# Stick-breaking attention: three score buffers, scores three heads ahead, taken between the exponents

## The reference, cut to what matters

```python
z = einsum('bhqd,bhkd->bhqk', qi, k) * scale
strict = kpos[None, :] < qpos[:, None]
u = where(strict, log_sigmoid(-z), 0.0)
tail = cumsum(u, axis=3, reverse=True) - u
w = where(strict, exp(log_sigmoid(z) + tail), 0.0)
out = einsum('bhqk,bhkd->bhqd', w, v)
```

## Time and profile before

| | us |
|---|---|
| median of 3 runs (lowest, highest) | 1932.29 (1927.04, 1932.38) |
| profiled execution: time, span | 1924.79, 1923.0 |
| busy PE / DVE / ACT, share of the span | 92% / 42% / 31% |
| first scores start, value rows start (in the span) | 929.08, 941.39 |
| loop over heads: first `rest`, last `values` matmul | 971.35, 1083.26 |

### The profile page before, as it was taken

The page is one execution under the profiler, slowest core; times in us unless marked ns, Lnnn a source line. Parts: engine busy times, 40 slices in busy tenths (PEclk is TensorE's granted clock), DMA queues, the critical chain, the costliest instruction groups (busy, mean ns, idle before and its releaser), DMA issues. The chain is left out here.

```text
span 1923.0 us, 27361 instructions
## 1 busy us (share of the span) xinstructions
PE 1759.9 (92%) x11698; PEld 1353.9 (70%) x11698; DVE 803.9 (42%) x1351; ACT 590.3 (31%) x988; POOL 61.5 (3%) x86
## 2 busy tenths in 40 slices
PE   6999989999989988738999899989999989999997
PEld 3883445666655655427765699889998889999886
DVE  3865566111110110144357467343236545444333
ACT  4323422100000000045557533443323333232222
POOL 1001000000000000020000000000000000000000
PEclk9999989999999999978899899899999999999999
DMA  9856525899999999951110111122233032322321
GB/s 371 273 170 192 228 102 197 336 427 425 427 428 427 426 427 427 416 191 41 38 45 23 45 45 35 54 67 88 88 97 123 1 99 89 109 89 88 110 88 44
DMA packets 111217, 355.38 MB, mean 185 GB/s; under 512 B 8663, under 2 KB 71405, under 8 KB 97399
## 3 DMA queue, kind: packets, MB, share of 16 engines
q1 hardware_dynamic: 106342, 343.89, 46.8%
q0 software_dynamic: 4224, 9.33, 1.4%
q10 hardware_dynamic: 530, 0.40, 0.1%
HBM read 330.21 MB, written 23.33 MB: 184 GB/s over the span
## 5 line engine op out<-in xcount | busy, mean ns | idle before, releaser
L1663 PE MATMUL psum<-parts_memory 128*128 128x256 f32 (+3 forms) x1136 | 346.8, 305 | 10.6 <-PEq L1882 3.3
L1665 PE MATMUL psum<-parts_memory 128*128 128x256 f32 (+3 forms) x1136 | 342.8, 302 | 0.0
L1664 PE MATMUL psum<-parts_memory 128*128 128x256 f32 (+3 forms) x1136 | 342.7, 302 | 0.0
L1562 DVE TENSOR_TENSOR parts_memory<-fixed,parts_memory 128x1024 fp32r<-128x1024 f32 x139 | 166.9, 1222 | 212.1 <-ACT parts_memory L1554 212.1
L1663 PEld LDWEIGHTS psum<-parts_memory 128*128 128x128 f32 x1136 | 218.0, 192 | 20.5 <-DVE parts_memory L1562 4.6
L1664 PEld LDWEIGHTS psum<-parts_memory 128*128 128x128 f32 x1136 | 217.9, 192 | 7.0
L1665 PEld LDWEIGHTS psum<-parts_memory 128*128 128x128 f32 x1136 | 217.5, 191 | 6.8
L1663 PE MATMUL psum<-mix_parts,parts_memory 128*128 128x256 f32 (+2 forms) x664 | 206.4, 311 | 4.7 <-PEq L2613 4.0
L1664 PE MATMUL psum<-mix_parts,parts_memory 128*128 128x256 f32 (+2 forms) x664 | 207.1, 312 | 0.0
L1665 PE MATMUL psum<-mix_parts,parts_memory 128*128 128x256 f32 (+2 forms) x664 | 206.4, 311 | 0.0
L1554 ACT ACTIVATE parts_memory<-fixed 128x1024 fp32r<-128x1024 f32 x139 | 143.2, 1055 | 120.7 <-PE psum L1665 109.6
(11 more groups left out here) (414 smaller groups left out, 2387.3 us busy)
## 6 DMA issues: line engine op xcount, KB each, us to landing
fixed<-in_w_exp_gate_dram SPq DMA_DIRECT2D x19, 2048.0 KB, 29.8
fixed<-in_w_exp_up_dram SPq DMA_DIRECT2D x19, 2048.0 KB, 31.1
fixed<-in_w_exp_down_dram SPq DMA_DIRECT2D x19, 2048.0 KB, 31.4
fixed<-in_w_in_dram SPq DMA_DIRECT2D x36, 1024.0 KB, 5.4
attention_memory<-in_w_exp_up_dram SPq DMA_DIRECT2D x14, 2048.0 KB, 31.1
attention_memory<-in_w_exp_down_dram SPq DMA_DIRECT2D x14, 2048.0 KB, 31.4
attention_memory<-in_w_exp_gate_dram SPq DMA_DIRECT2D x14, 2048.0 KB, 29.8
fixed<-in_w_mod_dram SPq DMA_DIRECT2D x8, 2048.0 KB, 9.0
```

What stands on the lines that cost most here:

```text
L1562: dve.tensor_tensor(out, raw, high.bitcast(F32), ALU.subtract).then_inc(self.low_ok, 1)
L1663: pe.matmul(out, x(0), w(0), start=start, stop=False)
L1664: pe.matmul(out, x(0), w(1), start=False, stop=False)
L1665: return pe.matmul(out, x(1), w(0), start=False, stop=stop)
```

## The change

There are now three buffers `zbuf` and none for `wbuf`, whose place they take together with one shared `tail`. The log term is written to `sbuf`, the softplus over it, and the exponents over the softplus, so that z stays whole until the weights are written over z. The pieces have their own banks (0, 1, 2, and 7 for "2", "3" and "m" together), `linear_query` moves from bank 7 to bank 6. `scores` run three heads ahead, all six pieces together, and DVE takes the scores of head h+2 between the exponents of head h. `linear_query` comes after `values`. The weights are made by two exps, and on ACT the log term of head h+2 comes before the outputs of head h are collected. POOL's memset covers three buffers. The core of the diff:

```diff
-    PIECES = (("0", 0, 0), ("x", 1, 1), ("1", 0, 0), ("2", 1, 1), ("3", 1, 7), ("m", 1, 2))
+    PIECES = (("0", 0, 0, 0), ("x", 1, 1, 0), ("1", 0, 2, 0), ("2", 1, 7, 0), ("3", 1, 7, 2 * P), ("m", 1, 7, 3 * P))
+    RESTS = (2, 3, 1, 0, "x", "m")
...
                 if r == 3:
-                    pe.wait_ge(z_sb, 11)
+                    pe.wait_ge(z_sb, 12)
...
             def linear_query(h):
                 w = parts.use(pe, GQ_AT + h // 2)
-                if h:
-                    pe.wait_ge(q_sb, h)
-                pe.wait_ge(z_sb, 6 * min(h + 1, HEADS - 1) + 5)
-                turned(pe, psum[:, 7, 0:HALF], w, x, (h % 2) * HALF, HALF).then_inc(q_ps, 1)
+                turned(pe, psum[:, 6, META:META + HALF], w, x, (h % 2) * HALF, HALF).then_inc(q_ps, 1)
...
-                    before = {0: 6 * h - 2, 2: 6 * h + 2, 4: 6 * h - 1, 5: 6 * h}.get(n, 0)
-                    if before > 0:
-                        pe.wait_ge(z_sb, before)
-                    if i == "3" and h >= 2:
-                        pe.wait_ge(q_sb, h - 1)
+                    if h and n < 4:
+                        pe.wait_ge(z_sb, 6 * (h - 1) + n + 1 if n < 3 else 6 * h)
...
                 pe.wait_ge(sp_ok, h + 1)
-                for n, i in enumerate((3, 2, 1, 0, "x", "m")):
-                    before = {0: 6 * h - 1, 1: 6 * h - 2, 2: 6 * h + 1, 3: 6 * h + 2, 4: 6 * h + 3, 5: 6 * h}[n]
-                    if before > 0:
-                        pe.wait_ge(arg_ok, before)
+                for n, i in enumerate(RESTS):
+                    bank = 3 + n % 2
+                    if h or n > 1:
+                        pe.wait_ge(arg_ok, 6 * h + n - 1)
...
             def values(h):
-                pe.wait_ge(w_ok, h + 1)
+                pe.wait_ge(w_ok, 2 * h + 1)
                 if h:
                     pe.wait_ge(pv_sb, 3 * h)
...
+                pe.wait_ge(w_ok, 2 * h + 2)
...
+                if h:
+                    pe.wait_ge(q_sb, h)
...
+            scores(2)
             for h in range(HEADS):
                 rest(h)
+                if h + 3 < HEADS:
+                    scores(h + 3)
+                values(h)
                 linear_query(h)
-                if h + 2 < HEADS:
-                    scores(h + 2, (0, 1))
-                values(h)
-                if h + 2 < HEADS:
-                    scores(h + 2, (2, 3, 4, 5))
...
+            def weights(h):
+                z, t = zbuf[:, h % 3, :], sbuf[:, h % 2, :]
+                act.wait_ge(arg_ok, 6 * h + 4)
+                act.activation(z[:, 0:Z_META], t[:, 0:Z_META], ACT.Exp).then_inc(w_ok, 1)
+                act.wait_ge(arg_ok, 6 * h + 6)
+                act.activation(z[0:META, Z_META:], t[0:META, Z_META:], ACT.Exp).then_inc(w_ok, 1)
...
             for h in range(HEADS):
-                act.wait_ge(arg_ok, 6 * h + 6)
-                act.activation(wbuf[:, h % 2, :], zbuf[:, h % 2, :], ACT.Exp).then_inc(w_ok, 1)
-                act.wait_ge(q_ps, h + 1)
-                act.activation(gq[:, h // 2, (h % 2) * HALF:(h % 2 + 1) * HALF], psum[:, 7, 0:HALF], ACT.Copy,
-                               scale=DK ** -0.5).then_inc(q_sb, 1)
+                weights(h)
+                if h + 2 < HEADS:
+                    log_term(h + 2)
                 take(h)
                 if h % 2:
                     parts.high(act, GQ_AT + h // 2 + W_SLOTS)
-                if h + 2 < HEADS:
-                    log_term(h + 2)
...
-                if h >= 2:
-                    dve.wait_ge(w_ok, h - 1)
+                if h >= 3 and n == 0:
+                    dve.wait_ge(pv_ps, 3 * (h - 2))
+                dve.wait_ge(z_ps, 6 * h + (n + 1 if n < 3 else 6))
...
             for h in range(HEADS):
-                exponents(h)
+                for n, pieces in enumerate(((), (0,), (1, 2), (3, 4, 5), (), ())):
+                    exponent(h, n)
+                    if h + 2 < HEADS:
+                        for piece in pieces:
+                            take_scores(h + 2, piece)
+                if h:
+                    add_later_keys(h - 1)
                 if h < 2:
                     parts.low(dve, GQ_AT + 2 + h)
                 elif h % 2 == 0:
                     parts.low(dve, GQ_AT + h // 2 - 1 + W_SLOTS)
                 if h + 1 < HEADS:
                     softplus(h + 1)
-                if h + 2 < HEADS:
-                    take_scores(h + 2, (0, 1))
-                add_later_keys(h)
-                if h + 2 < HEADS:
-                    take_scores(h + 2, (2, 3, 4, 5))
+            add_later_keys(HEADS - 1)
```

More of the change, by code:

```diff
@@ L1867, in stick_breaking @@
     o += 2560
[L1868 to L1871, removed]
+    tail = arena[:, o:o + Z_ALL]
+    o += Z_ALL
+    zbuf = arena[:, o:o + 3 * Z_ALL].rearrange("p (i n) -> p i n", i=3)
+    o += 3 * Z_ALL
     k2 = [src[:, at:at + K_ROWS] for src, at in [(big, 6336 + K_ROWS * n) for n in range(4)] +
@@ L1983, in values @@
             def values(h):
-                w = wbuf[:, h % 2, :]
-                pe.wait_ge(w_ok, h + 1)
+                w = zbuf[:, h % 3, :]
+                hc = slice(h * HD, (h + 1) * HD)
+                first, second = psum[0:HD, 5, :], psum[HD:2 * HD, 5, :]
+                pe.wait_ge(w_ok, 2 * h + 1)
                 if h:
                     pe.wait_ge(pv_sb, 3 * h)
[L1988 to L1995, removed]
+                for out, i in ((first, 0), (second, 1), (second, 2)):
+                    pe.matmul(out[:, i * P:], v[:, i, hc], w[:, Z_AT[i]:Z_AT[i] + (TT - i) * P], start=(i < 2), stop=False)
+                pe.wait_ge(w_ok, 2 * h + 2)
+                pe.matmul(first, v[:, TT, hc], w[:, Z_META + META:], start=False, stop=True).then_inc(pv_ps, 1)
+                pe.matmul(second[:, 3 * P:], v[:, 3, hc], w[:, Z_AT[3]:Z_AT[3] + P], start=False, stop=True).then_inc(pv_ps, 1)
+                if h:
+                    pe.wait_ge(q_sb, h)
                 pe.matmul(psum[0:HD, 6, 0:META], v[:, TT, hc], w[:, Z_META:Z_META + META], start=True, stop=True).then_inc(pv_ps, 1)
@@ L1999, in _ @@
             pe.wait_ge(taken, 16)
-            scores(0, range(6))
-            scores(1, range(6))
+            scores(0)
+            scores(1)
             for r in range(len(row_outputs)):
@@ L2134, in softplus, with exponent @@
                                            later_keys[:, Z_AT[i + 1]:Z_AT[i + 1] + (TT - i - 1) * P], ALU.add))
                 dve.engine_nop().then_inc(sp_ok, 1)
-            def exponents(h):
-                z = zbuf[:, h % 2, :]
-                for n, i in enumerate((3, 2, 1, 0, "x", "m")):
-                    dve.wait_ge(r_ps, 6 * h + n + 1)
-                    if i == "m":
-                        p, r = z[0:META, Z_META:Z_META + META], psum[0:META, 2, META:2 * META]
-                    elif i == "x":
-                        p, r = z[0:META, Z_META + META:], psum[0:META, 3, :]
-                    else:
-                        w = (TT - i) * P
-                        p, r = z[:, Z_AT[i]:Z_AT[i] + w], psum[:, 3 + n % 2, 0:w]
-                    dve.tensor_tensor(p, p, r, ALU.subtract).then_inc(arg_ok, 1)
+            def exponent(h, n):
+                z, s = zbuf[:, h % 3, :], sbuf[:, h % 2, :]
+                i, bank = RESTS[n], 3 + n % 2
+                dve.wait_ge(r_ps, 6 * h + n + 1)
+                if i == "m":
+                    rows, lo, w = META, Z_META, META
+                elif i == "x":
+                    rows, lo, w = META, Z_META + META, 512
+                else:
+                    rows, lo, w = P, Z_AT[i], (TT - i) * P
+                dve.tensor_tensor(s[0:rows, lo:lo + w], z[0:rows, lo:lo + w], psum[0:rows, bank, 0:w], ALU.subtract).then_inc(arg_ok, 1)
@@ L2150, in _ @@
             dve.wait_ge(zeroed, 2)
-            take_scores(0, range(6))
-            take_scores(1, range(6))
+            for h in range(2):
+                for n in range(6):
+                    take_scores(h, n)
             softplus(0)
```

81 lines of the change are left out of this document (40 added, 41 removed).

## The result

The changed kernel took 1916.55 us (median of 4 runs, 1911.46 to 1919.45) against 1931.78 for the kernel before, ratio 0.9924, 95% interval 0.9896 to 0.9951: faster by 0.8%. The forecast was 1924.1. Its direction was right, the gain too small (15 us in place of 8), and the time lies at the lower end of the range of 1917 to 1932 (0.9924 of the 1932.29 that the forecast started from is 1917.6).

A forecast was written before the change was run, and what follows sets the result against it. PE was taken as the bound, through waits and a slowed clock. Front 7.0 plus loop 1.2 gave 8.2 us, taken from the median 1932.29 us: 1924.1 us, range 1917 to 1932.

The forecast's parts named there:

- What bounds the kernel: PE, 92% busy; gains only where it is held up or slow, in the front and the loop over heads.
- The front: Scores of heads 0 and 1 before the value rows: no waits, full clock; 7.0 us saved, bounds 3.15 to 7.5.
- The loop: Loop over heads: only PE's waits change, 7.6 us in place of 8.8; 1.2 us saved.
- Item 1: Loop: PE's waits at the banks of scores, 0.43 us in head 0, go.
- Item 2: Loop: the wait inside rest stays but smaller, 0.42 us in each of eight heads, 3.4 us.
- Item 3: Loop: DVE's takes of scores, 2.7 us, fall into holes where it waited for rest; cost taken as 0.
- Item 4: Loop, heads 5, 6 and 7: nothing hides the weights before values; about 1.35 us each, 4.0 us together.
- Split exp: Loop, on ACT: the exp for 128 x 1280 takes 1.27 us, done before DVE's addition; costs nothing.
- The clock's term: Front: the part of the 7.0 us gain that comes from PE's clock staying at full; about 3.9 us.
- The clock part isn't won: Rival, front: only waits are saved, -3.2 - 1.2 us, some 1927.9 us; chance 0.17.
- The clock falls in the tail: Rival, heads 5 to 7: idle then half-column values drop the clock; -8.2 + 3.1, 1927.2 us; chance 0.13.
- DVE becomes the bound: Rival, loop: DVE's queue of exponents and takes delays softplus; at 4 us more a head, +5, 1937 us; chance 0.10.

The follow-up runs named there:

- e2_front: The kernel before with only the four-bank layout for the scores of heads 0 and 1, loop left old; 1917.49 us, ratio 0.9942.
- e4_warm: The kernel before plus three matmuls on all rows, into an unread bank, ahead of the three waits in the front; 1925.27 us, ratio 0.9976.
- e6_order: The changed kernel with rest in the old order 3, 2, 1 and an added DVE copy of softplus values; 1914.65 us, ratio 0.9937.
- e8_takes_late: The changed kernel, but DVE takes the scores of head h+2 after all exponents of head h; 1937.18 us, ratio 1.0052.
- e1_whole: The changed kernel once more, unaltered, with more rounds against the kernel before; 1919.41 us, ratio 0.9946.

## Why the prediction was right or wrong

**What bounds the kernel.** Right: PE, through waits and through the clock in one short stretch.

**The front.** Right, and the larger part, as said: 6.0 us with no wait, clock at full, the first value rows without the slow start. 7.0 was worked out, 7.2 measured (e2_front) against the trace that it was worked out from. The split into 3.15 us of waits and 3.9 us of clock is borne out by e4_warm, which wins 3.55 by the clock alone. Against the two later traces of before the same front is worth 8.7 us, since the clock's part is larger there.

**The loop.** 1.2 worked out, 1.4 measured. Item 1, the banks of scores: right. Item 2, the wait in `rest`: 0.42 us expected; by the starts 5.97 - 5.51 = 0.46, of which 0.29 shows as idle, and e6_order wins about 0.5 a head. Item 3, the takes in DVE's holes: right, and e8_takes_late shows what the opposite costs. Item 4, the weights in the last three heads: 1.35 expected, 1.5 measured; the code asks there for the first exp and the addition on DVE, and the trace names ACT's second exp, which ends at nearly the same time. A head was to last 14.1 us and lasts 13.94: the unhindered 13.66 were taken from head 0 of before and are 0.2 too long for the new order. There `linear_query` takes 988.78 - 985.75 = 3.03 us in place of 3.14 and `values` 985.75 - 983.82 = 1.93 in place of 2.01. Split exp: 1.27 and 0.64 us, as taken.

**The step that failed** is the last of the sum: "The median of the runs lies 7.5 us above that execution; the difference carries over". Executions of one kernel differ in the parts that the change doesn't touch, and this doesn't cancel between four runs here and four there: the first comparison showed 15 us, the longer one 10. Part of the 7.5 us may also lie in the changed stage itself. The clock's term, 3.9 us, was read from one execution, a mild one; in two further traces of before the fall costs 1.5 us more, which would be most of the 1.8 us that 10.4 is above 8.6. That the timed runs have the longer fall is likely by the traces and not shown. And that the first figure of the sum, 1916.6, agrees with the measured 1916.55 is luck: it stands for one execution that started from 1924.79, and the changed kernel's was 1911.46.

**The rivals.** The clock part isn't won: false, PEclk 1.00 in the front of every changed kernel. By the Trainium skill (TensorE: Matmul & The Clock Gate, section "Part 1: The HAM clock gate") the cold stretch varies from run to run. The traces agree for its length: in the front of before the clock is at half for 10.2, 13.6 and 13.6 us, and the stage is 157.7, 159.3 and 159.3 us. That it was missing altogether in some runs, on which the rival rested, no trace shows. The clock falls in the tail: false, 1.00 until the end of the loop, though e8_takes_late shows that nearly the same pattern brings it. DVE becomes the bound: false.

The Trainium skill (TensorE: Matmul & The Clock Gate), in the section "HAM oscillation — how this bites in real kernels", tells of a loop whose every turn has a wait that lets the clock fall again, so that the cost is paid once a turn. The trace of e8_takes_late agrees in the pattern, a fall in each of six heads, but not in the length of the waits: the waits in that section of the Trainium skill are 3 to 5 us long, and here five of the six falls came behind waits of 1.47 us.

## What to carry to other kernels

Before counting waits in the long loop, look for a short stretch in which the matrix engine's clock is at half: here three waits of 0.8 to 1.5 us next to half-filled matmuls cost as much again in clock as in waiting, and spreading six small outputs over four banks removed both. A producer that has been moved ahead must also be consumed in the consumer's own holes: the same takes cost nothing between the exponents, and 20 us behind them. When work that hid another engine's step is moved, look at the turns of the loop in which the new cover has run out; here it was the last three.

## What the runs showed of the hardware

Waits that look alike differ in what the clock makes of them. PE idle for 1.49 us between `rest` (all rows) and `values` (half the columns) left it at 1.00 in three heads. Idle for 1.47 us between `rest` and 5 us of scores and values, all on half the array, brought a fall in all five heads that still had scores (and 4.0 us idle ahead of `values` a sixth). What decides between them isn't settled; the kernels differ in how much half-filled work follows.

The part ahead of the stage is the same program in every kernel here, and yet the first scores start between 922.70 and 933.35 us. The granted clock is a part of it: ahead of the stage it is at half for 51 us in the earliest and 78 us in the latest of these (summed over 60 stretches of each trace). It isn't all, since two traces with the same 68 us (e1_whole and e6_order) start at 927.91 and 932.38. The spread is as large as the whole gain of the change, so one execution of each kernel can't measure it, while the length of the stage repeats to 0.1 us in the two traces of the changed kernel.
